# Pairing the key and value products of the prompt heads in a hybrid decoder step

## What is computed

```python
q = (cq @ w_qb)                                  # 64 plain + 32 rotary columns a head
kv = jnp.einsum('btr,rhd->bthd', ckv, w_kvb.reshape(KV_RANK, MLA_HEADS, QK_NOPE + V_DIM))
k = jnp.concatenate([kv[..., :QK_NOPE], broadcast(kr)], axis=-1)
s = jnp.einsum('bqkgd,btkd->bkgqt', q, k) * ATTN_SCALE
p = jax.nn.softmax(jnp.where(causal, s, -inf), axis=-1)
o = jnp.einsum('bkgqt,btkd->bqkgd', p, kv[..., QK_NOPE:])
```

## Time and profile before

| | us |
|---|---|
| median of three timed executions | 1696.12 |
| lowest and highest | 1691.58, 1697.44 |
| the profiled execution's own time | 1698.84 |
| its span on the core | 1697.3 |
| TensorE busy in it | 1617.9 (95%) |
| VectorE, ScalarE, GpSimd busy | 416.2, 278.1, 115.4 |
| mean granted TensorE clock | 0.975 of full |

### The profile page before, as it was taken

One profiled execution on the slowest core, in us unless ns is written; L12 is line 12 of the kernel. 1 busy time (PEld: TensorE's weight loads), 2 busy tenths in 40 slices (PEclk: granted clock), 3 DMA queues, 4 the chain that ended last, 5 costly groups with the idle time before them and its releaser, 6 DMA issues.

```text
span 1697.3 us, 20549 instructions
## 1 busy us (share of the span) xinstructions
PE 1617.9 (95%) x7924; PEld 1016.3 (60%) x7924; DVE 416.2 (25%) x974; ACT 278.1 (16%) x621; POOL 115.4 (7%) x195
## 2 busy tenths in 40 slices
PE   7999988999999999987998999999999999999998
PEld 3544544678888878776786454544445454544444
DVE  2233322220000055689475000010000000010113
ACT  2222333110000022364503100000000000000001
POOL 0001424000000010100012000010000000010000
PEclk9999999999999999998998899999999999999999
DMA  9666963444434654544469799999999999999998
GB/s 373 259 207 207 397 205 88 149 125 149 143 103 132 193 187 127 151 140 136 154 225 347 239 347 394 385 383 388 387 392 384 380 385 392 386 376 397 392 381 326
DMA packets 236763, 462.94 MB, mean 273 GB/s; under 512 B 13455, under 2 KB 112812, under 8 KB 227414
## 3 DMA queue, kind: packets, MB, share of 16 engines
q1 hardware_dynamic: 222112, 413.93, 67.9%
q0 software_dynamic: 12048, 46.53, 8.2%
q10 hardware_dynamic: 2512, 1.23, 0.2%
HBM read 445.97 MB, written 15.88 MB: 272 GB/s over the span
## 4 chain that ended last, share of the span: by engine, by line
PE 87%; DVE 7%; ACT 2%; issue 2%; DMA 1%; POOLq 0%; POOL 0%; SPq 0%; DVEq 0%; ACTq 0%
PE bank L1359 18%; PE bank L1016 10%; PE bank L1046 9%; PE bank L1400 9%; PE bank L1374 9%; PE bank L1412 5%; PE bank L1060 5%; PE bank L755 3%; PE bank L789 1%; PE bank L842 1%; DVE ysp L2028 1%; DVE prod L2027 1%; PE bank L1094 1%; PE bank L847 1%; PE bank L726 1%
## 5 line engine op out<-in xcount | busy, mean ns | idle before, releaser
L1359 PE MATMUL bank<-ring,hg 128*128 128x512 f32 (+1 forms) x624 | 253.8, 564 | 0.7 <-ACT hg L1691 0.7
L1359 PEld LDWEIGHTS bank<-ring,hg 128*128 128x128 f32 x624 | 118.8, 191 | 131.4 <-issue 129.0
L1046 PE MATMUL bank<-hT,ring 128*128 128x264 f32 x704 | 156.9, 386 | 0.3 <-ACT hT L1471 0.3
L1046 PEld LDWEIGHTS bank<-hT,ring 128*128 128x128 f32 x704 | 133.7, 190 | 23.4 <-issue 0.6
L2314 DVE TENSOR_TENSOR actH<-sgH,bank 128x512 f32<-128x512 f32 (+1 forms) x24 | 15.4, 643 | 464.0 <-PE bank L1359 464.0
L1016 PE MATMUL bank<-hT,ring 128*128 128x264 f32 x512 | 117.2, 390 | 1.6 <-ACT hT L1471 1.3
L1400 PE MATMUL bank<-ring,turnH 128*128 128x512 f32 x256 | 114.3, 599 | 3.3 <-ACT turnH L1716 3.3
L1016 PEld LDWEIGHTS bank<-hT,ring 128*128 128x128 f32 x512 | 98.1, 192 | 19.4 <-issue 2.1
L1374 PE MATMUL bank<-ringx,hg 128*64 128x256 f32 x832 | 93.0, 381 | 0.0
L1400 PEld LDWEIGHTS bank<-ring,turnH 128*128 128x128 f32 x256 | 47.2, 190 | 67.8 <-issue 66.9
L1060 PE MATMUL bank<-actT,ring 128*128 128x264 f32 x352 | 79.1, 386 | 0.6 <-DVE actT L1931 0.6
(11 more groups left out here) (526 smaller groups left out, 1793.0 us busy)
## 6 DMA issues: line engine op xcount, KB each, us to landing
ring<-in_moe_w_down SPq DMA_DIRECT2D x70, 1024.0 KB, 13.9
ring<-in_moe_w_up SPq DMA_DIRECT2D x59, 1024.0 KB, 13.2
ring<-in_moe_w_gate SPq DMA_DIRECT2D x55, 1024.0 KB, 13.5
ring<-in_w_ada SPq DMA_DIRECT2D x48, 1024.0 KB, 9.7
ringx<-in_moe_w_gate SPq DMA_DIRECT2D x37, 1024.0 KB, 13.2
ringx<-in_moe_w_up SPq DMA_DIRECT2D x33, 1024.0 KB, 14.1
ring<-in_ssm_w_in SPq DMA_DIRECT2D x20, 1024.0 KB, 5.3
ringx<-in_moe_w_down SPq DMA_DIRECT2D x20, 1024.0 KB, 13.9
```

The lines of the kernel that those rows point to most:

```text
L1046: m = mm(bank[2 * w + q][:, 0:T], slot8(tl)[:, k, q * P:(q + 1) * P], hT[:, k, :], start=k == 0, stop=k == DC - 1)
L1359: m = mm(bank[b_][:, 0:width], hg[:, k, 0:CAPH], w[:, kk, :], start=k == 0, stop=k == DC - 1)
```

## The change

Keys: the products of two heads are issued together, in the even head's turn, alternating between the lower and the upper half of a bank; the bank is 2 or 5 by pairs. The rotation then has bank 4 alone and waits for VectorE to have finished the head before. Values: `values` takes a pair of heads and alternates between the halves in the same way; it is called after the even heads from 2 on and at the end. `ptbuf` gets four buffers.

```diff
-    ptbuf = late[:, 768:1536].rearrange("p (u t) -> p u t", u=2)
+    ptbuf = late[:, 768:2304].rearrange("p (u t) -> p u t", u=4)
...
         def head_back(h):
             pe.wait_ge(s["q_copied"], h + 1)
-            if h >= 2:
-                pe.wait_ge(s["q_ready"], h - 1)
-            elif h == 0:
+            if h:
+                pe.wait_ge(s["q_ready"], h)
+            else:
                 pe.wait_ge(s["ltok_copied"], 3)
-            mm(bank[4 + h % 2][64:96, 0:T], cst[64:96, C_ROT:C_ROT + ROPE], qT[64:96, h, :], start=True, stop=True).then_inc(s["q_rotated"], 1)
+            mm(bank[4][64:96, 0:T], cst[64:96, C_ROT:C_ROT + ROPE], qT[64:96, h, :], start=True, stop=True).then_inc(s["q_rotated"], 1)
...
-            if h >= 2:
-                pe.wait_ge(s["k_copied"], h - 1)
-            for k in range(KC):
-                m = mm(bank[2][64 * (h % 2):64 * (h % 2) + NOPE, 0:TP], wkvb[:, k, h * P:h * P + NOPE], projT[:, QC + k, 0:TP], start=k == 0, stop=k == KC - 1)
-            m.then_inc(s["k_done"], 1)
+            if h % 2 == 0:
+                if h >= 4:
+                    pe.wait_ge(s["k_copied"], h - 2)
+                for k in range(KC):
+                    for hh in (h, h + 1):
+                        m = mm(bank[(2, 5)[h // 2 % 2]][64 * (hh % 2):64 * (hh % 2) + NOPE, 0:TP], wkvb[:, k, hh * P:hh * P + NOPE], projT[:, QC + k, 0:TP],
+                               start=k == 0, stop=k == KC - 1, skip_group_check=True)
+                m.then_inc(s["k_done"], 1)
...
-        def values(h):
-            pair = h // 2
-            out = bank[pair % 2][(h % 2) * 64:(h % 2) * 64 + 64, :]
-            pe.wait_ge(s["pt_copied"], h + 1)
+        def values(pair):
...
+            pe.wait_ge(s["pt_copied"], 2 * pair + 2)
             if pair >= 2:
                 pe.wait_ge(s["o_copied"], pair - 1)
-            mm(out[:, 0:TP], vtok[:, 0, h * VD:(h + 1) * VD], ptbuf[:, h % 2, 0:TP], start=True, stop=False, skip_group_check=True)
-            mm(out[:, P:TP], vtok[:, 1, h * VD:(h + 1) * VD], ptbuf[:, h % 2, TP:TP + P], start=False, stop=True,
-               skip_group_check=True).then_inc(s["o_done"], 1)
+            for t, cols in ((0, slice(0, TP)), (1, slice(P, TP))):
+                for u in range(2):
+                    h = 2 * pair + u
+                    m = mm(bank[pair % 2][64 * u:64 * u + 64, cols], vtok[:, t, h * VD:(h + 1) * VD], ptbuf[:, h % 4, TP * t:TP * t + (TP, P)[t]],
+                           start=t == 0, stop=t == 1, skip_group_check=True)
+            m.then_inc(s["o_done"], 2)
...
-            if h >= 1:
-                values(h - 1)
+            if h % 2 == 0 and h:
+                values(h // 2 - 1)
         ada1_turn(2)
-        values(H - 1)
+        values(H // 2 - 1)
...
-            act.wait_ge(s["k_done"], h + 1)
-            f(kT[0:NOPE, h, :], bank[2][64 * (h % 2):64 * (h % 2) + NOPE, 0:TP], ACT.Copy).then_inc(s["k_copied"], 1)
+            act.wait_ge(s["k_done"], h // 2 + 1)
+            f(kT[0:NOPE, h, :], bank[(2, 5)[h // 2 % 2]][64 * (h % 2):64 * (h % 2) + NOPE, 0:TP], ACT.Copy).then_inc(s["k_copied"], 1)
...
-            if h >= 2:
-                act.wait_ge(s["o_done"], h - 1)
-            f(ptbuf[:, h % 2, :], bank[6][:, 0:384], ACT.Copy).then_inc(s["pt_copied"], 1)
+            if h >= 4:
+                act.wait_ge(s["o_done"], 2 * (h // 2) - 2)
+            f(ptbuf[:, h % 4, :], bank[6][:, 0:384], ACT.Copy).then_inc(s["pt_copied"], 1)
...
-            v.tensor_tensor(ropet[64:96, :], bank[4 + h % 2][64:96, 0:T], sin, ALU.mult)
+            v.tensor_tensor(ropet[64:96, :], bank[4][64:96, 0:T], sin, ALU.mult)
```

## The result

| | kernel before | changed kernel |
|---|---|---|
| timed executions, median | 1694.2 us (4 runs) | 1673.33 us (4 runs) |
| lowest and highest | 1691.58, 1697.44 | 1671.97, 1680.18 |
| ratio, 95% interval | | 0.9884 [0.985, 0.9918] |
| profiled execution, own time | 1698.84 | 1671.97 |
| its span | 1697.3 | 1670.4 |

The forecast sum was 14.6 us; the medians differ by 20.9, the profiled spans by 26.9. Ratios are taken over all the runs of a kernel, so they differ a little from the quotient of two medians.

A forecast was written before the change was run, and what follows sets the result against it. TensorE's order was taken to bound the head loop and scores stage, with transfers a near second limit in the latter. Savings of 8.2 (keys) + 6.8 (values) - 0.4 (new wait) = 14.6 us gave 1681.5 us, range 1677 to 1689.

The forecast's parts named there:

- The forecast sum: Head loop and scores stage: keys save 8.2 us, values 6.8, less 0.4 for a new wait: 14.6 us.
- The new wait at the end: End of scores stage: the last L767 must wait for VectorE's copy of the last tile's rows, 0.4 us given back.
- against the median of the runs, 1696.12 ... it is 1681.5 us: Whole kernel: 14.6 us taken off the median of three timed runs, 1696.12, gives 1681.5 us.
- 1.5 to 4 us for the dips: Whole kernel: allowance in the range for small clock dips elsewhere, giving 1677 to 1689 us.
- the pauses at a change of shape: Key and value groups: a fixed 0.10 us for each group, beside 0.109 us per unit of 256 columns.
- the line through two rows: Expert layers (64 units, 7.06 us) and sample attention (16, 1.84): 0.109 us a unit plus 0.10 a group.
- Short groups pairing badly: Key and value groups: first and last pass may run alone; only 9.8 us saved, 1686.3 us; chance 0.11.
- The 2.38 of the Trainium skill: Key and value groups: 2.38 times for three column tiles, estimated as 1.59 for two halves, would give some 1686.4 us.
- No overlap at all: Key and value groups: halves don't overlap, only shape changes go away, about 2 us less 0.4: 1694.5 us; chance 0.04.
- Transfers setting the beat: Scores stage: transfers limit it; if nothing is gained there, only the keys' 8.2 us remain, 1687.9 us; chance 0.06.
- the floor at 64.6: Scores stage: its 25.4 MB at 393 GB/s take 64.6 us, leaving 4 us of slack below the forecast 68.6.
- Slower by the clock: Scores stage: clock may drop repeatedly as the 0.57 us wait weighs more; 1703 us after 50 us at half; chance 0.04.

The follow-up runs named there:

- the version with the values moved: Changed kernel with a pair's values issued ahead of the probabilities' transposes in even heads, instead of behind them: median 1671.39 us, ratio 0.9873.

## Why the prediction was right and wrong

*Direction and mechanism: right.* TensorE's order bounded both stages, the halves overlap, and the gain passed through the page loads into everything behind. The bank arrangement cost nothing, as a run shows. The new wait at the end was there, 0.36 us for a forecast 0.4. Behind the start of the scores stage the clock did not fall again (0.97 in the mean of the stage, 0.95 before).

*The step that failed first: "against the median of the runs, 1696.12 ... it is 1681.5 us".* I took the sum off a median of three runs and took that for the kernel's level. Two of those three runs, and the profiled one, lie at the upper level, 1695 us or more. Medians of 14, 17 and 17 later runs are 1690.07, 1692.19 and 1691.33 us. This base was 4 to 6 us too high, and that is the larger part of the 8.2 us of the miss. Runs at the upper level have a mean clock of at most 0.977 (a few others have it too), and with products in the pauses of the routing part they do not come up. That points to the routing clock; that it is this stretch alone is not shown, since one profiled execution had it and lay only 2.0 us above its kernel's median. The profile of before showed the stretch at clock 0.50 from 920 to 940 us. I read the clock only around the touched stages, and gave "1.5 to 4 us for the dips" where the gathering products of this one alone took 6.4 us more.

*The term of the sum that was mis-sized: the pauses at a change of shape.* The sum put a fixed 0.10 us on each group and took odd heads to lose just what stood between the rows. Measured per pair:

| | forecast | measured |
|---|---|---|
| keys of a pair | 0.97 us | 1.01 us |
| two heads of the head loop | 8.85 us | 8.76 us |
| values of a pair | 0.75 us | 0.80 us |
| two heads of the scores stage | 7.8 us | 7.66 us |

Both groups are a little slower than the line through two rows gave. What outweighs it is the odd heads: with the keys gone, the turned weights follow the queries 0.10 us sooner than the keys did (1.41 against 1.51 us), and with the values gone, the scores follow the transposes 0.11 us after the last, where the values followed after 0.20. The first scores product then takes 0.44 us up to the next (166.62 to 167.06), where behind the values it takes 0.53 (170.74 to 171.27). Per pair this leaves 0.09 us more than forecast in the head loop (1.12 for 1.03) and 0.12 in the scores stage (0.97 for 0.85). So the two stages, run one at a time, gave 8.8 and 7.4 us for a forecast 8.2 and 6.4: 1.6 us that the sum lacks. The changed kernel's profile has 0.6 more in the scores stage, from a shorter stretch at the lower clock behind the first scores: the first conditioning tile took 1.85 us before and 1.24 after.

```profile
153.40 1.24 PE L755 MATMUL bank<-ring,scT 128*32 128x512 f32 x8
```

The Trainium skill (TensorEngine Tiling (Array Packing), Key Properties) says that changing the tiling mode drains the engine; the odd heads, 0.10 us shorter than the products taken away, agree with it. It does not cover everything here: the turned weights also write 64 rows, and straight behind the queries they show no such pause, 0.22 us from the last query pass (98.58) to them (98.80), where the keys wait 0.32 (102.39 to 102.71).

*The rivals.* Short groups pairing badly: refuted by 1.01 and 0.80 us. The 2.38 of the Trainium skill (TensorE: Matmul & The Clock Gate, Measured speedup vs the span model) for three tiles, as an estimate 1.59 for two: not borne out, since the group of eight passes takes 1.01 us over two halves and 1.87 in one, 1.85 times. The 1686.4 us that I gave for it was not worked out right either: 3.60 us of keys and values a pair, divided by 1.59, save 1.34, and 8 x 1.34 - 0.4 = 10.3 us gives 1685.8. No overlap at all: what it would look like is the run with both heads in one half. Transfers setting the beat: not in the changed kernel, where TensorE waits for no tile at 363 GB/s in the scores stage. In the version with the values moved it waits 1.5 us for one, in a stage of 63.9 us; I had put the floor at 64.6, so the slack that I worked out was about right. Slower by the clock: refuted for the scores stage; low stretches elsewhere moved the totals of both kernels.

*What stays open.* The touched stages give 8.8 + 7.4 to 8.0 = 16.2 to 16.8 us, the timed medians with the routing products 18.1. The remaining 1 to 2 us lie within the spread of those runs, or in low stretches in untouched code, of which the two profiles with the routing products show one worth 3.4 us ahead of the routing part. Whether the change favours such differences or they fall by chance, no run tells. That the lower clock in the routing part comes in some executions and not in others is made likely by the two levels of the timed runs; no kernel has two profiles that show it, and why it should is open.

## What to carry to other kernels

Products with 64 rows of output cost TensorE about half when products for the other 64 partitions stand in the same unbroken group (here 1.01 us for two heads' keys, after 2 x 1.00); look for pairs of heads whose products are separated by something of another shape, and count the pauses of about 0.1 us around each group that you do away with. Before setting a forecast against a median, look over the whole profile for stretches at clock 0.50: one such stretch, 6.4 to 7.7 us here, can weigh as much as one of the two halves of the change. When a wait on TensorE is left, see whether ready work can be issued ahead of it; here that took 2.6 us off the stage in the profile, after a new wait for the transfers had taken back 1.5.

## What the runs showed that I had not expected

Within a group the order of issue between the two halves does not matter: four passes of one head followed by four of the other took 1.02 us, in turns 1.01, and the first passes of both heads start together. The Trainium skill (TensorE: Matmul & The Clock Gate, What overlaps and what doesn't) has matmuls start and end strictly in program order; the trace does not agree with it for two column halves. In that order the second head's first pass could start no earlier than the first head's fourth, some 0.7 us into the group, and in the value group its 256-column passes could not come ahead of the first head's 128-column ones.

A few products that compute nothing, put into the pauses of the routing part, took the kernel before from a median of 1692.19 to 1688.55 us, ratio 0.9975 [0.996, 0.999].
